# One encoder kernel, its DeltaNet core: the order of work on all engines set anew, the output copied out of its bank, the masks folded into the decay sums

## The chip, the core and the metric

The kernel is one program on one core of a Trainium2 chip. Five engines work side by side and meet only at semaphores: TensorE (PE, matrix products into PSUM), VectorE (DVE), ScalarE (ACT), GpSimd (POOL) and the queue of SyncE (SP), which issues the loads. An engine runs its own instructions strictly in the order in which they are written, so an instruction that waits holds back all that stand behind it. The metric is the time of one execution on the device in microseconds (us).

## What is computed

Two encoder layers on 256 tokens of width 2048, in float32. Layer 0 mixes tokens with a bidirectional gated DeltaNet (32 value heads on 16 key heads, two directions), layer 1 with a convolution module, and each is followed by a SwiGLU block. The change touches only the DeltaNet's recurrence. Cut to what matters (one direction; the other is the same on flipped time):

```python
g = jnp.cumsum(chunks(g), axis=-1)
decay = jnp.exp(jnp.where(incl, g[..., :, None] - g[..., None, :], -jnp.inf))
lower = jnp.where(strict, jnp.einsum('nbhid,nbhjd->nbhij', k_beta, k) * decay, 0.0)
sol = lax.linalg.triangular_solve(eye + lower, rhs, left_side=True, lower=True)
a_qk = jnp.einsum('nbhid,nbhjd->nbhij', q, k) * decay
# per chunk: v_new = u - w S ; o = (q exp(g)) S + a_qk v_new ; S = S cd + k_tail^T v_new
o = rmsnorm(o_f + o_b, norm_w) * jax.nn.silu(z)
return o.reshape(B, T, V_DIM) @ out_w
```

## The kernel before, in words

All projections before and after the core are dense products with split float32 weights (lines 651 to 670). Between them stands the **core**, a loop written out over 16 key heads. One "head" here is one key head with its two value heads and both directions, that is four problems `c` = 2 x direction + value head, over two blocks `t` of 128 tokens. With blocks of 128 the solve is done by block inversion: inverses of the 32x32 diagonal blocks (`inv`, made earlier, loaded per head) are joined to 64x64 and then to 128x128 inverses `t64`.

For each head the stages are, with the names that the prediction uses:

- **sums** (DVE, line 1415, 12 instructions): `exb` = row sums `rr` plus a column sum from `ncum`, cut off at 0. **exponentials** (ACT, line 1946, four for the keys `d0`, four for the queries `d1`): `dec` = exp(`exb`).
- **kq** (PE, line 885): k k^T and k q^T into the PSUM bank `psg[:, 0]`. **masks** (DVE, lines 1387 and 1389): `mk` = that bank times triangular 0/1 masks. **masked** (DVE, line 1395, four for keys, four for queries): `dec` times `mk`. **lm** (DVE, line 1406, four): the part of it that joins 32 to 64.
- **W** (PE, line 864), **wt** (ACT, line 1961, two copies), **tn** (line 908) and **t** (line 872) on PE, **tnb** (line 1445) and **t64** (line 1449) on DVE, **y** (line 940), **yb** (ACT, line 1983), **t2** (line 947), **t128** (ACT, line 1991, two copies): these join the inverses.
- **rv** (ACT, line 1979, eight): values times beta. **u0** (PE, line 856), **uu0** (ACT, line 1941, a copy), **X** (PE, line 895), **r2** (DVE, line 1422), **u1** (PE, line 856), **uu1** (ACT, line 1941): the solution of the first block, its effect on the second, the second.
- **o** (PE, line 925, 12 products, shown as x24): the output of both directions into the bank `ps_o`. **squares** (ACT, line 1956) read `ps_o`; **oms** (DVE, lines 1426 and 1429), 12 small operations on POOL (lines 2264 to 2270) for the inverse root, **og** (DVE, line 1439) reads `ps_o` again and multiplies by root and gate. **T** (PE, line 641) transposes `og`, **oT** (ACT, line 1986) stores it.

The order is written by hand. In its step `h` the loop makes the inverses of head h, solves and outputs head h-1, and finishes the statistics of head h-2; with two steps to drain it takes 18 steps. PE waits ahead of **o** for `og_done` of the head before, since `ps_o` is one bank:

```python
pe.wait_ge(uc_done, 2 * b + 2)
pe.wait_ge(aq_done, b + 1)
pe.wait_ge(og_done, b)
```

SP loads per head `rr` (1 MB, a broadcast), q and k, v, the gate z, and `inv` as eight small transfers (line 508), the last after `t64_done`, since `inv` is one buffer. The core is entered when the last gate product is copied out, and left when the last `oT` is stored; then the weights of the output projection are loaded into the buffers that the core had borrowed.

Of the kernel before, what the change touches and what calls it, by code (L numbers as in the profile page):

```python
# [64 lines left out]
def build(nc, x_in, c_in, ada_w, ada_b, norm_w, gdn_in_w, gdn_conv_w, gdn_A_log, gdn_dt_bias,  # L65
# [31 lines left out]
    with stack:  # L97
# [96 lines left out]
        masks = sb("masks", [P, 2, 2, 3, P], at=p2a)  # L194
# [8 lines left out]
        dec = sb("dec", [P, 2, 4, 2, 3, P], at=p2a)  # L203
        osq = sb("osq", [P, 4, P], at=p2a)
# [8 lines left out]
        sb("apart", [P, 756], at=p2a)  # L213
# [49 lines left out]
        ps_b = pst[:, 2:4, :].rearrange("p a (b m) -> p (a b) m", m=P)  # L263
# [75 lines left out]
        mk_done = sem("mk_done")  # L339
# [10 lines left out]
        u_done, uc_done = sem("u_done"), sem("uc_done")  # L350
# [23 lines left out]
        C_TRI, C_SINV, C_CONST = 5, 7, 22  # L374
# [41 lines left out]
        def _(sp):  # L416
# [94 lines left out]
            def core_loads(h):  # L511

                if h + 2 < HQ:
                    sp.wait_ge(kq_done, h + 2)
                    load_qk(h + 2)
                    sp.wait_ge(ex_done, h + 2)
                    load_rr(h + 2)
                if 1 <= h <= HQ:
                    if h > 1:
                        sp.wait_ge(og_done, h - 1)  # L520
                    else:
                        sp.wait_ge(z_out, 16 * NZ)
                    load_z(h - 1)
                if h + 1 < HQ:
                    sp.wait_ge(rv_done, 2 * (h + 1))
                    load_v(h + 1)
                    sp.wait_ge(t64_done, h + 1)
                    load_inv(h + 1)
# [29 lines left out]
            sp.wait_ge(inv_out, 48)  # L558
            sp.dma_start(x[:, :, :], x_in[0].rearrange("(t p) d -> p t d", p=P)).then_inc(x_land, 16)
            for h in range(HQ + 1):  # L560
                core_loads(h)
# [75 lines left out]
        def _(pe):  # L637
# [210 lines left out]
            def step(h):  # L848
                par, b = h % 2, h - 1
                M, A, B, C = h + 1 < HQ, h < HQ, 0 <= b < HQ, 0 <= h - 2  # L850
                q = 1 - par

                def u_stage(o):
                    for c in range(4):
                        t = o if c < 2 else 1 - o
                        i = mm(ps_a[:, c, :], t64[:, q, c, t, :], rv[:, q, o, c, :], start=True, stop=True)  # L856
                    i.then_inc(u_done, 1)

                def w_stage(d):

                    pe.wait_ge(lm_done, 2 * h + d + 1)
                    for c in (2 * d, 2 * d + 1):
                        for t in range(TT):
                            i = mm(ps_w[:, 2 * c + t, :], lm[:, c, t, :], inv[:, slot_of(0, c), t, :], start=True, stop=True)  # L864
                    i.then_inc(w_done, 1)

                def t_stage(d):

                    pe.wait_ge(wt_done, 2 * h + d + 1)
                    for c in (2 * d, 2 * d + 1):  # L870
# [4 lines left out]
                if B:  # L875
                    pe.wait_ge(rv_done, 2 * b + 1)
                    pe.wait_ge(t128_ok, 2 * (b + 1))
                    u_stage(0)
                if M:
                    pe.wait_ge(qk_land, 32 * (h + 2))  # L880
                    pe.wait_ge(mk_done, h + 1)
                    if h == 0:
                        pe.wait_ge(ps_read, S_GO)
                    for jt in range(2):
                        i = mm(psg[:, 0, jt, :], qk[:, 0, jt * P:(jt + 1) * P],  # L885
                               qk[:, :, :].rearrange("p k t -> p (k t)"), start=True, stop=True)
                    i.then_inc(kq_done, 1)
                if A:
                    pe.wait_ge(inv_land, 128 * (h + 1))
                    w_stage(0)  # L890
                    w_stage(1)
                if B:
                    pe.wait_ge(uc_done, 2 * b + 1)
                    for c in range(4):
                        i = mm(ps_b[:, c, :], dec[:, q, c, 0, 1, :], uu[:, 0, c, :], start=True, stop=True)
                    i.then_inc(x_done, 1)
                if A:
                    t_stage(0)
                    t_stage(1)
                if B:  # L900
                    pe.wait_ge(r2_done, 2 * (b + 1))
                    u_stage(1)
                if A:

                    for c in range(4):
                        f = first(c // 2)
                        for t in range(TT):
                            i = mm(ps_n[f, c % 2, t, :], inv[f, slot_of(1, c), t, f], wt[f, c, t, f], start=True, stop=True)
                    i.then_inc(tn_done, 1)
                if B:  # L910
# [17 lines left out]
                if C:  # L928
                    pe.wait_ge(og_done, h - 1)
                    pe.wait_ge(oT_done, h - 2)  # L930
                    for v in range(2):
                        for t in range(TT):
                            i = tr(ps_oT[:, v, t * P:(t + 1) * P], og[:, 2 * t + v, :])
                    i.then_inc(ot_done, 1)
                if A:
                    pe.wait_ge(tn_ok, 2 * (h + 1))
                    for c in range(4):
                        f, s = first(c // 2), second(c // 2)
                        for t in range(TT):
                            i = mm(ps_y[s, c % 2, t, :], dec[f, par, c, 0, 2 * t, s], tnb[f, c % 2, t, :], start=True, stop=True)  # L940
                    i.then_inc(y2_done, 1)
                    pe.wait_ge(y2_ok, h + 1)
                    pe.wait_ge(t64_done, h + 1)
                    for c in range(4):
                        f, s = first(c // 2), second(c // 2)
                        for t in range(TT):
                            i = mm(ps_n[f, c % 2, t, :], yb2[s, c % 2, t, :], t64[s, par, c, t, s], start=True, stop=True)
                    i.then_inc(t2_done, 1)
            for h in range(HQ + 2):
                step(h)  # L950
# [127 lines left out]
        def _(dve):  # L1078
# [296 lines left out]
            mkf = mk[:, :, :, :, :].rearrange("p d k s m -> p d k (s m)")  # L1375
            mmf = masks[:, :, :, :, :].rearrange("p d k s m -> p d k (s m)")
# [3 lines left out]
            def step(h):  # L1380
                par, b = h % 2, h - 1
                M, A, B, C = h + 1 < HQ, 0 <= h < HQ, 0 <= b < HQ, 0 <= h - 2
                p = 1 - par

                def mask(d):
                    kqf = kq0 if h < 0 else kqs
                    tt(mkf[:, d, :, d * P:(d + 2) * P], kqf[:, d], mmf[:, d, :, d * P:(d + 2) * P], MUL)
                    n = 2 - 2 * d
                    return tt(mkf[:, d, :, n * P:(n + 1) * P], kqf[:, 1 - d, :, (1 - d) * P:(2 - d) * P],
                              mmf[:, d, :, n * P:(n + 1) * P], MUL)  # L1390

                def masked(kind, done):
                    for c in range(4):
                        f = dec[:, par, c, kind].rearrange("p s m -> p (s m)")
                        i = tt(f, f, mk[:, c // 2, kind].rearrange("p s m -> p (s m)"), MUL)
                    i.then_inc(done, 1)

                if A:
                    dve.wait_ge(d0_done, h + 1)
                    dve.wait_ge(mk_done, h + 1)  # L1400
                    masked(0, la_done)
                    dve.wait_ge(la_done, h + 1)
                    dve.wait_ge(w_done, 2 * h)
                    for d in range(2):
                        for v in range(2):
                            i = tt(lm[:, 2 * d + v, :, :], dec[:, par, 2 * d + v, 0, 0:3:2, :],
                                   m64[:, d:d + 1, :].broadcast_to([P, TT, P]), MUL)
                        i.then_inc(lm_done, 1)
                if M:

                    dve.wait_ge(rr_land, 16 * (h + 2))
                    dve.wait_ge(d1_done, h + 1)
                    for c in range(4):
                        for seg, t, kind, tj in ((0, 0, 0, 0), (2, 1, 0, 1), (1, 1 - c // 2, 1, c // 2)):
# [883 lines left out]
```

## Time and profile before

| what | us |
|---|---|
| median of 3 runs (lowest, highest) | 3267.35 (3266.91, 3268.53) |
| the profiled execution, its own time | 3268.26 |
| its span | 3266.7 |
| PE busy in the span | 2953.7 |
| DVE busy | 2264.2 |
| ACT busy | 1275.6 |
| one head of the core, from one **o** to the next | 20.41 |
| first **W** of the core to the end of the last **oT** | 743.99 to 1083.06 |

Times inside the profile are counted from the start of the span. A row of instructions has its start, its length, engine, line and tiles; a `x24` behind it counts the instructions merged into it. A float32 product shows as two matmul records, so 12 products are x24. "PEclk" is the clock granted to TensorE, as a share of full speed: 1.00 is 2.4 GHz and 0.50 is 1.2 GHz.

### The profile page before, as it was taken

The page shows a single profiled execution, that of the slowest core. Times are in us where ns is not written, and L with a number is a line of the kernel's source. Part 1 is how long each engine was busy: PE and PEld are TensorE (multiplying, and loading weights), DVE is VectorE, ACT ScalarE, POOL GpSimd, SP SyncE. Part 2 cuts the span into 40 slices and gives each one's busy share as a digit, 9 for nine tenths or more (in the row PEclk, how much of TensorE's full clock was granted, in tenths as well). Part 3 has the DMA queues.
Part 4 walks back from the last instruction along what each step waited for, and adds up shares of the span by engine and source line. Part 5 has one row for each costly group of instructions (what it writes and reads, how often), then busy time and mean ns, then how long its engine had stood idle before and what let it go on. Part 6 is the DMA issues. An engine that isn't in the chain of part 4 may idle for free.

```text
span 3266.7 us, 37727 instructions
## 1 busy us (share of the span) xinstructions
PE 2953.7 (90%) x13796; PEld 2382.1 (73%) x13796; DVE 2264.2 (69%) x2388; ACT 1275.6 (39%) x1383; POOL 163.6 (5%) x313
## 2 busy tenths in 40 slices
PE   1699999997777698899999999799987999999998
PEld 1577778876777577788888888644576888888886
DVE  6588868967776478787877877529966655555555
ACT  2356634335554334333333333421144333333333
POOL 0011111320111000000000000000000000000000
PEclk8799999998998799999999999899998999999998
DMA  9666766674332598798888888354334766656653
GB/s 376 227 224 238 244 218 217 206 235 146 104 104 65 182 372 327 274 341 308 310 308 315 337 315 333 99 167 149 122 121 155 252 206 216 201 201 203 214 204 122
DMA packets 322173, 731.61 MB, mean 224 GB/s; under 512 B 48128, under 2 KB 64336, under 8 KB 293648
## 3 DMA queue, kind: packets, MB, share of 16 engines
q1 hardware_dynamic: 316256, 709.85, 61.5%
q0 software_dynamic: 5808, 20.35, 1.8%
q8 instruction: 62, 1.02, 0.1%
q14 instruction: 47, 0.39, 0.0%
HBM read 710.45 MB, written 19.69 MB: 224 GB/s over the span
## 4 chain that ended last, share of the span: by engine, by line
PE 82%; DVE 7%; DMA 4%; ACT 3%; issue 2%; POOL 2%; DVEq 0%; SPq 0%; ACTq 0%
PE psg L664 44%; PE psg L670 22%; PE psg L651 5%; DMA aring<-in_ada_w 3%; PE psn L925 2%; PE pst L641 1%; PE psn L691 1%; PE psg L864 1%; DVE wlo L1086 1%; PE psg L885 1%; PE psn L1049 1%; DVE y L1598 1%; PE psn L641 1%; DMA wraw<-in_gdn_out_w 1%; PE pst L856 1%
## 5 line engine op out<-in xcount | busy, mean ns | idle before, releaser
L1722 ACT ACTIVATE whi<-wraw 128x2048 fp32r<-128x2048 f32 x408 | 781.8, 1916 | 1319.7 <-PE psg L670 1163.6
L1086 DVE TENSOR_TENSOR wlo<-wraw,whi 128x2048 fp32r<-128x2048 f32 x408 | 935.2, 2293 | 482.9 <-ACT whi L1722 481.0
L664 PE MATMUL psg<-whi,h_hi 128*128 128x512 f32 x2304 | 731.3, 399 | 33.6 <-DVE h_lo L1678 13.2
L664 PE MATMUL psg<-whi,h_lo 128*128 128x512 f32 x2304 | 719.9, 394 | 0.0
L670 PE MATMUL psg<-wlo,h_hi 128*128 128x512 f32 x2304 | 572.1, 391 | 12.0 <-DVE wlo L1086 12.0
L664 PEld LDWEIGHTS psg<-whi,h_hi 128*128 128x128 f32 x2304 | 435.5, 191 | 127.9 <-issue 25.6
L670 PEld LDWEIGHTS psg<-wlo,h_hi 128*128 128x128 f32 x2304 | 433.6, 188 | 104.0 <-DVE wlo L1086 13.9
L664 PEld LDWEIGHTS psg<-whi,h_lo 128*128 128x128 f32 x2304 | 439.5, 191 | 93.9
L1096 DVE SCALAR_TENSOR_TENSOR aacc<-aring,cond,aacc 128x2048 f32<-128x2048 f32 x150 | 352.0, 2346 | 6.6 <-DMA aring<-in_ada_w 6.0
L651 PE MATMUL psg<-wraw,aring 128*128 128x512 f32 x512 | 221.1, 592 | 0.0
L664 PE MATMUL psg<-whi,g_hi 128*128 128x512 f32 x704 | 219.9, 394 | 0.0
L664 PE MATMUL psg<-whi,g_lo 128*128 128x512 f32 x704 | 219.3, 393 | 0.0
L651 PEld LDWEIGHTS psg<-wraw,aring 128*128 128x128 f32 x512 | 96.7, 190 | 118.6 <-issue 118.6
L670 PE MATMUL psg<-wlo,g_hi 128*128 128x512 f32 x704 | 173.9, 389 | 0.0
L664 PEld LDWEIGHTS psg<-whi,g_hi 128*128 128x128 f32 x704 | 134.1, 191 | 28.0
L664 PEld LDWEIGHTS psg<-whi,g_lo 128*128 128x128 f32 x704 | 133.9, 190 | 28.2
L1517 DVE TENSOR_TENSOR y<-psg,y 128x1024 f32<-128x1024 f32 x88 | 107.6, 1223 | 66.9 <-PE psg L670 66.1
L670 PEld LDWEIGHTS psg<-wlo,g_hi 128*128 128x128 f32 x704 | 132.2, 188 | 27.5
L1598 DVE SCALAR_TENSOR_TENSOR y<-glu,vec,y 128x242 f32 (+14 forms) x360 | 139.8, 475 | 0.0
L1310 DVE SCALAR_TENSOR_TENSOR cv<-pst,vec,cv 128x254 f32<-128x254 f32 (+1 forms) x256 | 117.3, 480 | 23.3 <-DVE cv L1310 1.7
L925 PE MATMUL psn<-wraw,dec 128*128 128x128 f32 x384 | 71.8, 372 | 45.2 <-DVE og L1439 45.2
L2251 POOL DMA_DIRECT2D d_cw<-cwc x4 | 4.7, 1178 | 2096.4 <-DVE cwc L1170 2095.5
(251 smaller groups left out, 2600.0 us busy)
## 6 DMA issues: line engine op xcount, KB each, us to landing
aring<-in_ada_w SPq DMA_DIRECT2D x192, 1024.0 KB, 7.0
wraw<-in_ffn_in_w SPq DMA_DIRECT2D x176, 1024.0 KB, 6.8
wraw<-in_gdn_in_w SPq DMA_DIRECT2D x96, 1024.0 KB, 5.1
wraw<-in_ffn_out_w SPq DMA_DIRECT2D x88, 1024.0 KB, 5.2
wraw<-in_cf_pw_w SPq DMA_DIRECT2D x48, 1024.0 KB, 5.5
wraw<-in_gdn_out_w SPq DMA_DIRECT2D x32, 1024.0 KB, 8.5
wraw<-d_rr SPq DMA_DIRECT2D x16, 1024.0 KB, 4.7
x<-in_x SPq DMA_DIRECT2D x2, 2048.0 KB, 9.2
```

The source lines that it names most:

```text
L641: return nc.tensor.transpose(dst, src, ident[:, :])
L651: i = mm(ps[:, t, :], a[:, kc, t * P:(t + 1) * P], wraw[:, slot, j * NSL:(j + 1) * NSL], start=first and j == 0, stop=last and j == len(kc ...
L664: mm(ps[:, t, 0:width], a[:, kc, t * P:(t + 1) * P], wh, start=first and j + n == 0, stop=False)
L670: i = mm(ps[:, t, 0:width], a_hi[:, kc, t * P:(t + 1) * P], wl, start=False, stop=last and j == len(kcs) - 1)
L691: i = mm(psn[:, 0, kc:kc + 1], acc[:, kc * P:(kc + 1) * P], ones[:, 0:1], start=True, stop=True)
L925: i = mm(ps_o[:, 2 * t + v, :], dec[:, q, c, 1, seg, :], uu[:, o, c, :], start=n == 0, stop=n == len(terms) - 1)
L1086: tt(wlo[:, j % 2, :], wraw[:, j % 4, :], whi[:, j % 2, :].bitcast(F32), SUB).then_inc(w_lo, 1)
L1096: stt(acc, ring[:, par, :], c, acc, MUL, ADD).then_inc(a_used, 1)
L1310: i = stt(dst, src, w, dst, MUL, ADD)
L1517: tt(yj, psg[:, (s0 + par) % 2], yj, ADD).then_inc(ps_read, 1)
L1598: i = stt(dst, src, w, dst, MUL, ADD)
L1722: av(whi[:, j % 2, :], wraw[:, j % 4, :], ACT.Copy).then_inc(w_hi, 1)
```

## The change

Only the core changes; the amount of PE work is the same. Five things are done.

**1. Five steps a head.** The statistics of the output move a step later, and the transpose **T** one more: step `s` of the new loop makes the inverses of head s, outputs head s-1, does the statistics of head s-2 and transposes head s-3. The first solution **u0** moves from the start of the next step to the end of its own. There are 19 steps on PE and ACT. In SP's queue the loads are in a new order, and the reload of `x` (2 MB), which stood ahead of the loop, stands behind step 3.

PE, one step in the middle of the core, before (the names are tiles: `psn<-wraw,dec` is **o**, `psn<-ident,og` is **T**, `psg<-wraw,lm` is **W**, `psg<-qk` is **kq**):

```order
L864 MATMUL psg<-wraw,lm 128x128 x8
L895 MATMUL pst<-wraw,dec 128x128 x4
L872 MATMUL psg<-wraw 128x128 x8
L856 MATMUL pst<-rv,t 128x128 x4
L908 MATMUL pst<-wraw 64x64 x8
L925 MATMUL psn<-wraw,dec 128x128 x12
L641 MATMUL psn<-ident,og 128x128 x4
L940 MATMUL pst<-tnb,dec 64x64 x8
L947 MATMUL pst<-t,yb 64x64 x8
L856 MATMUL pst<-rv,t 128x128 x4
L885 MATMUL psg<-qk 128x512 x2
```

PE, one step in the same place of the changed program:

```order
L869 MATMUL psg<-wraw,lm 128x128 x8
L641 MATMUL psn<-ident,og 128x128 x4
L882 MATMUL pst<-wraw,dec 128x128 x4
L893 MATMUL pst<-wraw 64x64 x8
L897 MATMUL psg<-wraw 128x128 x8
L903 MATMUL psg<-qk 128x512 x2
L911 MATMUL pst<-tnb,dec 64x64 x8
L856 MATMUL pst<-rv,t 128x128 x4
L922 MATMUL pst<-t,yb 64x64 x8
L940 MATMUL psn<-wraw,dec 128x128 x12
L856 MATMUL pst<-rv,t 128x128 x4
```

The same products stand in another order: **T** behind **W**, **tn** ahead of **t**, **kq** in the middle of the step, **u1** between **y** and **t2**, and **o** next to last.

DVE, one step before (`exb<-` are the sums, `og<-` the gated output):

```order
L1395 TENSOR_TENSOR dec<-dec,mk 128x384 x4
L1406 TENSOR_TENSOR lm<-dec,m 128x256 x4
L1415 TENSOR_SCALAR exb<-wraw,ncum 128x2x128 x12
L1422 TENSOR_TENSOR rv<-pst,rv 128x256 x2
L1426 TENSOR_SCALAR oms<-oms 128x4
L1429 TENSOR_SCALAR oms<-oms 128x4
L1395 TENSOR_TENSOR dec<-dec,mk 128x384 x4
L1439 SCALAR_TENSOR_TENSOR og<-psn,oms,zt 128x128 x4
L1445 TENSOR_TENSOR tnb<-pst,wraw 64x256 x2
L1449 TENSOR_TENSOR t<-psg,wraw 128x512 x2
L1387 TENSOR_TENSOR mk<-psg,masks 128x2x256
```

DVE, in the changed step, behind the sums (which are eight SCALAR_TENSOR_TENSOR and four TENSOR_SCALAR):

```order
L1385 TENSOR_SCALAR exb<-wraw,ncum 128x2x128
L1398 TENSOR_TENSOR dec<-dec,psg 128x2x256
L1398 TENSOR_TENSOR dec<-dec,psg 128x2x128
L1398 TENSOR_TENSOR dec<-dec,psg 128x2x256
L1398 TENSOR_TENSOR dec<-dec,psg 128x2x128
L1431 TENSOR_TENSOR tnb<-pst,wraw 64x256 x2
L1435 TENSOR_SCALAR oms<-oms 128x4
L1439 TENSOR_SCALAR oms<-oms 128x4
L1446 TENSOR_TENSOR rv<-rv,pst 128x256 x2
L1452 TENSOR_TENSOR t<-psg,wraw 128x512 x2
L1398 TENSOR_TENSOR dec<-dec,psg 128x2x256
```

Behind these rows come the rest of the keys, `lm`, and `og` as the last of the step. The masks are gone as instructions, and `og` no longer stands between the queries and `tnb`.

**2. The output is copied.** ACT copies `ps_o` to a buffer `os` as its first work of the next step; the squares and `og` read `os`. PE's wait for `og` ahead of **o** becomes a wait for that copy (`oc_ok`).

**3. Decay sums held twice.** `exb` has two halves, by the parity of the head, so the sums of a head wait for the query exponentials of the head before last.

**4. Masks as a bound.** A triangle `tri0` with 0 inside and -1000 outside is the upper bound of the sum, so that the exponential is 0 outside. `dec` is then multiplied by the products straight from PSUM.

**5. X goes to the bank `ps_a`**, from which `uu0` was copied, since `ps_b` shares its bank with **tn** and **y**. The factors -1 and the scale of the queries move from the masks into `m64`, **r2**, **yb** and the copy `os`.

```diff
-        mk = sb("mk", [P, 2, 2, 3, P], at=p2a)
-        exb = sb("exb", [P, 4, 2, 3, P], at=p2a)
+        exb = sb("exb", [P, 2, 4, 2, 3, P], at=p2a)
+        os = sb("os", [P, 4, P], at=p2a)
...
+            def decay_sums(h):
+                dve.wait_ge(rr_land, 16 * (h + 1))
+                if h > 1:
+                    dve.wait_ge(d1_done, h - 1)
+                for c in range(4):
+                    for seg, t, kind, tj in ((0, 0, 0, 0), (2, 1, 0, 1), (1, 1 - c // 2, 1, c // 2)):
+                        to, row = exb[:, h % 2, c, :, seg, :], rr[:, 2 * c:2 * c + 2, t * P:(t + 1) * P]
+                        col = ncum[:, kind, tj, c, h:h + 1]
+                        if seg == 1:
+                            i = ts(to, row, col, 0.0, ADD, MIN)
+                        else:
+                            i = stt(to, row, col, tri0[:, c // 2:c // 2 + 1, :].broadcast_to([P, 2, P]), ADD, MIN)
+                i.then_inc(ex_done, 1)
+
+            def decayed(h, kind, done):
+                kqf = kqs if h else kq0
+                for d in range(2):
+                    n = 2 - 2 * d
+                    f = dec[:, h % 2, 2 * d:2 * d + 2, kind].rearrange("p c s m -> p c (s m)")
+                    for to, kq in ((f[:, :, d * P:(d + 2) * P], kqf[:, d, kind, :]),
+                                   (f[:, :, n * P:(n + 1) * P], kqf[:, 1 - d, kind, (1 - d) * P:(2 - d) * P])):
+                        i = tt(to, to, kq.unsqueeze(1).broadcast_to(list(to.shape)), MUL)
+                i.then_inc(done, 1)
...
+                if C:
+                    act.wait_ge(o_done, g + 1)
+                    if g:
+                        act.wait_ge(og_done, g)
+                    av(os[:, :, :], ps_o, ACT.Copy, scale=float(P) ** -0.5).then_inc(oc_ok, 1)
...
                 if B:
-                    pe.wait_ge(uc_done, 2 * b + 2)
+                    pe.wait_ge(uc1_done, b + 1)
                     pe.wait_ge(aq_done, b + 1)
-                    pe.wait_ge(og_done, b)
+                    if b:
+                        pe.wait_ge(oc_ok, b)
...
+            def core_loads(s):
+                if s + 2 < HQ:
+                    sp.wait_ge(ex_done, s + 2)
+                    load_rr(s + 2)
+                if s + 1 < HQ:
+                    sp.wait_ge(rv_done, s + 1)
+                    load_v(s + 1)
+                    sp.wait_ge(t64_done, s + 1)
+                    load_inv(s + 1)
+                if s + 2 < HQ:
+                    sp.wait_ge(kq_done, s + 2)
+                    load_qk(s + 2)
...
+                sel(out=tri0[:, d, :], in_=tri0[:, d, :], compare_op=ALU.is_ge, fill=-1000.0, base=0,
+                    pattern=[[sign, P]], channel_multiplier=-sign)
```

## Rows read from the trace of the kernel before

**Rows 1.** Busy time of the engines in whole heads; columns: PE, PEld, DVE, ACT, POOL, clock, DMA.

```profile
799.58:820.00 20.42, 15.94 (x139) 14.34 (x138) 14.53 (x40) 10.90 (x32) 3.19 (x12) 0.92 0.36 104
```

**Rows 2.** Chain of work that ended last, one head: start, length, what.

```profile
785.95 4.54 PE psn L925 x24
790.49 0.44 PE psn L641 x4
790.93 0.91 PE pst L940 x16
...
792.29 0.98 PE pst L947 x16
...
794.22 1.13 PE pst L856 x8
795.35 1.72 PE psg L885 x4
797.06 1.78 PE psg L864 x16
798.85 0.91 PE pst L895 x8
...
806.36 4.54 PE psn L925 x24
```

**Rows 3.** The same chain in the second step, whose o waited for no og.

```profile
759.71 1.78 PE psg L864 x16
...
762.39 1.79 PE psg L872 x16
764.17 0.89 PE pst L856 x8
765.07 0.89 PE pst L908 x16
765.96 2.88 PE psn L925 x24
```

**Rows 4.** Busy time and clock, columns as in rows 1, of short stretches.

```profile
766.00:769.00 3.00, 3.00 (x28) 2.88 (x29) 2.94 (x6) 2.03 (x7) 0.00 (x0) 1.00 0.13 46
909.40:910.40 1.00, 1.00 (x6) 1.00 (x6) 1.00 (x3) 0.00 (x0) 0.00 (x0) 0.50 0.89 269
```

**Rows 5.** Who waited for whom in the core: us in total, times, longest.

```profile
PE psn L925 <- DVE og L1439: 45.2, 15, 3.1
PE pst L856 <- ACT t L1991: 15.4, 16, 1.0
```

**Rows 6.** Instructions in order of time, ACT, DVE and SP, in one head.

```profile
895.39 0.78 ACT L1991 ACTIVATE t<-pst 64x256 f32<-64x256 f32 x2 [0.56 <-PE pst L947]
896.19 1.76 ACT L1946 ACTIVATE dec<-exb 128x384 f32<-128x384 f32 x4
898.06 3.24 DVE L1415 TENSOR_SCALAR exb<-wraw,ncum 128x256 f32<-128x256 f32 x12 [2.66 <-ACT dec L1946]
910.33 0.68 DVE L1387 TENSOR_TENSOR mk<-psg,masks 128x512 f32<-128x512 f32 x1
910.45 3.79 SPq L508 DMA_DIRECT2D wraw<-d_inv  x8
912.38 1.97 DVE L1395 TENSOR_TENSOR dec<-dec,mk 128x384 f32<-128x384 f32 x4
```

**Rows 7.** The same view of DVE later, two SBUF tensors and a column scalar.

```profile
2199.87 6.36 DVE L1598 SCALAR_TENSOR_TENSOR y<-glu,vec,y 128x251 f32 x16
```

**Rows 8.** DMA issues of the core: count, KB each, median us to landing.

```profile
wraw<-d_inv SPq DMA_DIRECT2D x63, 32.0 KB, 2.0
```

**Rows 9.** The chain at the core's last W and its end.

```profile
1040.38 1.79 PE psg L864 x16
...
1075.16 1.15 ACT osq L1956 x8
...
1082.45 0.61 ACT oT L1986
```

More of the change, by code:

```diff
@@ L557, in _ @@
             load_rr(1)
[L558 to L561, printed above, removed]
+            for s in range(HQ + 1):
+                core_loads(s)
+                if s == 3:
+                    sp.wait_ge(inv_out, 48)
+                    sp.dma_start(x[:, :, :], x_in[0].rearrange("(t p) d -> p t d", p=P)).then_inc(x_land, 16)
             sp.wait_ge(oT_done, HQ)
@@ L927, in step @@
                     i.then_inc(o_done, 1)
[L928 to L934, printed above, removed]
-                if A:
[L936 to L950, printed above, removed]
+                if A:
+                    pe.wait_ge(rv_done, s + 1)
+                    pe.wait_ge(t128_ok, s + 1)
+                    u_stage(s, 0, u0_done)
+            for s in range(HQ + 3):
+                step(s)
             pe.wait_ge(oT_done, HQ)
@@ new lines, in keys @@
+            def keys(h):
+                dve.wait_ge(kq_done, h + 1)
+                dve.wait_ge(d0_done, h + 1)
+                decayed(h, 0, la_done)
+                dve.wait_ge(la_done, h + 1)
+                if h:
+                    dve.wait_ge(w_done, 2 * h)
+                for d in range(2):
+                    for v in range(2):
+                        i = tt(lm[:, 2 * d + v, :, :], dec[:, h % 2, 2 * d + v, 0, 0:3:2, :],
+                               m64[:, d:d + 1, :].broadcast_to([P, TT, P]), MUL)
+                    i.then_inc(lm_done, 1)
@@ new lines, in queries, with step @@
+            def queries(h):
+                dve.wait_ge(kq_done, h + 1)
+                dve.wait_ge(d1_done, h + 1)
+                decayed(h, 1, aq_done)
+            def step(s):
+                par, b, g = s % 2, s - 1, s - 2
+                M, A, B, C = s + 1 < HQ, s < HQ, 0 <= b < HQ, 0 <= g < HQ
+                if M:
+                    decay_sums(s + 1)
+                if A:
+                    if s:
+                        queries(s)
+                    dve.wait_ge(tn_done, s + 1)
+                    for d in range(2):
+                        f, slot = first(d), slot_of(0, 2 * d)
+                        i = tt(tnb[f], ps_n[f], inv[f, slot:slot + 2, :, f], ADD)
+                    i.then_inc(tn_ok, 1)
+                if C:
+                    dve.wait_ge(osq_done, g + 1)
+                    ts(oms[:, 1, :], oms[:, 0, :], 1.0 / P, RMS_EPS, MUL, ADD).then_inc(oms_done, 1)
+                    dve.wait_ge(oms_done, 2 * g + 1)
+                    if g:
+                        dve.wait_ge(ors_done, 12 * g)
+                    ts(oms[:, 2, :].bitcast(I32), oms[:, 1, :].bitcast(I32), -0.5, float(0x5f3759df), MUL, ADD
+                       ).then_inc(oms_done, 1)
@@ L1459, in _ @@
+            decay_sums(0)
+            keys(0)
+            queries(0)
             dve.wait_ge(inv_out0, 48)
@@ L1461, in _ @@
             dve.wait_ge(kk_out, 16 * 4 * 4)
-            for h in range(HQ + 2):
-                step(h)
+            dve.wait_ge(z_out, 16 * NZ)
+            for s in range(HQ + 2):
+                step(s)
             dve.wait_ge(oT_done, HQ)
@@ L1968, in step @@
-                if B:
-                    solution(1)
+                if C:
+                    act.wait_ge(oc_ok, g + 1)
+                    if g:
+                        act.wait_ge(oms_done, 2 * g)
+                    for n in range(4):
+                        i = av(osq[:, n, :], os[:, n, :], ACT.Square, accum_out=oms[:, 0, n:n + 1])
+                    i.then_inc(osq_done, 1)
+                if E:
+                    act.wait_ge(ot_done, e + 1)
+                    av(oT[:, 2 * e:2 * e + 2, :], ps_oT, ACT.Copy).then_inc(oT_done, 1)
@@ L2000, in _ @@
             act.wait_ge(kk_out, 16 * 4 * 4)
-            for h in range(HQ + 2):
-                step(h)
+            for s in range(HQ + 3):
+                step(s)
             hi(G_GO, G_GO)
```

308 lines of the change are left out of this document (130 added, 178 removed).

## The prediction

> **What bounds the kernel now.** I read the core first, since only it changes: its heads take 20.41 us each, from one **o** to the next [rows 2], and PE is busy for 15.94 us of such a stretch, DVE for 14.53, ACT for 10.90 [rows 1]. So no engine is full. The chain of waits says who holds the period: PE itself at every stage but three. The PE stages of one head add up, in the order of the chain, to 4.54 (**o**) + 0.44 (**T**) + 0.91 (**y**) + 0.98 (**t2**) + 1.13 (**u0**) + 1.72 (**kq**) + 1.78 (**W**) + 0.91 (**X**) [rows 2] + 1.79 (**t**) + 0.89 (**u1**) + 0.89 (**tn**) [rows 3] = 15.98, which is the busy time of rows 1. The 4.4 us left are three waits of every head: **o** for **og** 45.2/15 = 3.0, **u0** for the copies **t128** 15.4/16 = 1.0 [rows 5], and **t2** for **yb**, from the end of **y** at 790.93 + 0.91 to 792.29, 0.5 [rows 2].
>
> The first of these waits costs more than itself. **o** takes 4.54 us in a head that waited [rows 2] but 2.88 us in the second step, which waited for nothing [rows 3]. The granted clock tells why: it is at 0.50 (1.2 GHz) within an **o** that followed such a wait, and at 1.00 (2.4 GHz) in the undisturbed one [rows 4]. Waits of 0.5 and 1.0 us are followed by stages at their full-clock length (**t2** 0.98, **u0** 1.13) [rows 2]. So the wait for **og** costs 3.0 + (4.54 - 2.88) = 4.7 us a head, of 20.4.
>
> **The change, part by part.**
>
> *The copy and the later statistics.* **o** of head s-1 now waits for the copy of head s-2, which ACT makes early in the step, some 10 us ahead. The chain squares, oms, POOL, og stays as long as it was but ends in a later step, where only **T** of the step after next needs it. Gain 4.7 us a head; added are 0.60 us of ACT for the copy (a copy of 128x512 from PSUM, like `oT` [rows 9]), beside PE's work. If the cover were gone, the copy would cost its 0.60.
>
> *The other two waits.* **u1** (0.89) now runs between **y** and **t2**, longer than the 0.5 us that **yb** needs; **o** (2.88) runs between **t2** and **u0**, longer than the 1.0 us of **t128**. Gain 0.5 + 1.0 = 1.5. What is late next: **X** stands 1.78 + 0.44 us behind the end of **u0** and needs **uu0**. ACT, from the end of **o**, does `d1` 1.76 [rows 6], `os` 0.60, **uu0** 0.60, so **uu0** is ready at about 3.0; **X** may start at 1.13 + 1.78 + 0.44 = 3.35. It fits by 0.3.
>
> *PE after it.* 15.98 - 1.66 = 14.3 us a head at full clock. This is the floor.
>
> *DVE.* Removed: the masks, 912.38 - 910.33 = 2.05 us, and the masked products, 2 x 1.97 = 3.94, and the old sums, 3.24 [rows 6]. Added: the products straight from PSUM. They have the shapes of the masks (512, 256, 512, 256 elements, one operand from the same bank) and are needed once for the keys and once for the queries, so 2 x 2.05 = 4.10. The new sums: four as before at 3.24/12 = 0.27, and eight with two tensors from SBUF and a column scalar. The nearest row has 16 such of 251 elements in 6.36 us, 0.40 each [rows 7]. 4 x 0.27 + 8 x 0.40 = 4.28. DVE is then busy for 14.53 - 2.05 - 3.94 - 3.24 + 4.10 + 4.28 = 13.7 us. From below the new sums cannot be under the 3.24 of the simpler ones; from above they cost twice the old 0.27 each, 8 x 0.54 + 1.08 = 5.4, DVE 14.8. I take 4.28: that row differs from the new one only in the broadcast operand.
>
> On this the Trainium skill speaks against the change. Its page "VectorE: DVE Perf Modes", section "Mode 2×_2P — use both read ports for one tensor", says that a float32 operation with one SBUF tensor may use both read ports and run at two elements a cycle, which one with two tensors cannot. Taken as a factor of two it gives the 5.4 us above; the rows have 0.40 against 0.27, since much of so short an instruction is fixed.
>
> *Double `exb`.* Before, the sums waited 2.66 us for the exponentials [rows 6]. With two halves they wait for nothing near. It moves no engine that is the bound by itself, but without it DVE would not fit into 14.3.
>
> *ACT.* 10.90 + 0.60 = 11.5 us busy. But ACT stands in a ring with PE: end of **o**, all of ACT's step up to **uu1** but not **t128** (0.78 [rows 6]), then **o** again: 11.5 - 0.78 + 2.88 = 13.6, with two hand-overs 13.8. Under PE, by half a microsecond.
>
> *SP and the load of `inv`.* One buffer, loaded between **t64** and the next **W**. From the end of **t64**, 3.79 us of issue [rows 6] and 2.0 to the landing [rows 8]: 5.8. In a step that starts with **W**, **t** ends at 1.78 + 0.44 + 0.91 + 0.89 + 1.79 = 5.8; DVE adds 1.2 to 1.3 for **t64**, and if it comes late from **r2** up to 1.5 more: end 7.1 to 8.6, landing 12.9 to 14.4. **W** is due at 14.3. This is the closest of all, and it is new: before, the issue began at 910.45 [rows 6], 9.1 us ahead of the next **W** (which stood 11.1 us behind the start of **o** [rows 2], near 919.6). At zero to 0.1 us of waiting I leave it inside the joints below. `rr` is asked for after the sums and has some 10 us to land; q and k are issued behind `inv` now, and are needed most of a step later.
>
> *Joints.* Three loops (PE 14.3, DVE 13.7, ACT and PE 13.8) and the load at 14.4 touch each other, each hand-over costing 0.05 to 0.1. I take 0.3 for them, between 0 and 1: a **period of 14.6 us**.
>
> *Start.* The first **W** waits for the same: sums of head 0, exponentials, keys. DVE now makes the queries of head 0 before it goes on (+2 us), but loses the masks. The second step's **W** started at 759.71 [rows 3]; it hangs on **t64** of head 0 and the `inv` load, and I keep 759.7, 1 us either way. The 2 MB for `x` no longer go ahead of the first loads; they land beside step 4.
>
> *End.* Before, from the last head's **W** to the last `oT`: 1082.45 + 0.61 - 1040.38 = 42.7 us [rows 9]. After: the rest of that step 14.6; then **uu0** 0.6, **X**, **r2** 0.8, **u1**, **uu1** 0.6, **o** with the hand-overs, 7 us at full clock, 12 at half, taken 9.0; then `os` 0.6 and from squares to `oT` as now, 1083.06 - 1075.16 = 7.9. Sum 32.1. The third pipeline stage costs one step of latency at the end, and that is in it. The load of the next weights behind it stays.
>
> *Sum.* 759.7 + 14 x 14.6 + 32.1 = 996.2 against 1083.1: 86.9 us gained. The profiled execution took 3268.26, so 3181.4; the median of the runs shown is 0.9 lower, so **3180.5**.
>
> **The rivals.** Each microsecond on the period is 15 us of time.
>
> *B, DVE becomes the bound.* If the new sums cost 5.4, or the products from PSUM more than the masks did, DVE needs 14.8, and with its own waits (for `d0`, for POOL between oms and og) 15.2 to 16. Speaks for it: DVE is at 13.7 of 14.6 in strict order. Against: rows 7. Time 3190 to 3202.
>
> The price of 5.4 is the one that the rule of the skill's VectorE page gives if it is taken as a plain factor of two.
>
> *C, the load of `inv` becomes the bound.* If it lands 2 us later than its median, PE idles some 1 to 2 us ahead of every **W**, and the clock may fall again as it did behind the wait for **og**, 1.7 more: period 17 to 18, time 3217 to 3232. Speaks for it: eight small issues in series, next to no slack. Against: the 1 MB of `rr` is no longer in flight at the same time.
>
> *D, slower than before.* The place is PE's order itself: eleven stages, nearly each behind another engine's semaphore. If the small waits between them kept the granted clock at 0.50 for the whole step, the 14.3 us of work would take 28.6: 3180.5 + 15 x 14.3 = 3395. It decides against the change from the point where a step has more than 2 x (20.4 - 14.6) = 11.6 us at half clock. Against it: the short waits of today are followed by stages at full length.
>
> *E, it does not do what it says.* DVE's fixed order could pass the old wait on: **kq** now waits for the queries, **y** for `tnb`, both behind the sums. If DVE were a whole chain behind, the period would stay near 20 and the time near 3262.
>
> **How the numbers follow.** Forecast (period 14.1 to 15): 0.58, 3173 to 3187. B: 0.22. C: 0.12. D: 0.03. E: 0.05, of which a fifth ends within 0.2% of before. The range takes in the forecast with the period at 14.1 and a short end (3168), all of B, and what lies between B and C up to a period of 16.7 (3212); left out are the rest of C, D and E. A measurement of this kernel tells about 0.2%, 6.5 us, from no change. Faster by more: 0.95; within: 0.01; slower: 0.04.
>
> **What would show it.** In the changed profile: **o** at about 2.9 us with a granted clock near 1.00 through the core; no wait of PE for **og** except at the end; heads at 14.6 us; the new sums at 0.40 each and products from PSUM like the masks; PE ahead of **W** waiting for the load by tenths. If instead DVE is busy without a gap and **kq** or **y** wait for it, B is right; if **W** waits for a DMA by a microsecond or more, C. The forecast is wrong if **o** stays at 4.5 without a wait ahead of it: then its length was not the clock's, and 1.7 x 15 = 25 us of the gain are missing.

## The result

The changed kernel takes 3178.53 us (median of 4 runs, 3175.08 to 3181.21) against 3267.75 us for the kernel before (4 runs): ratio 0.9725, 95% interval 0.9713 to 0.9737, 89 us less. The profiled execution took 3177.12 us, 91.1 less than the one of before. Two executions ran quite otherwise, one of `b_order` (3859 us, mean granted clock 0.74) and one of the kernel before (6827 us), and stand in none of the ratios.

Nearly all of the gain is in the core: from the first **W** to the end of the last **oT** it took 743.99 to 1083.06 before and takes 742.40 to 991.10 now, 90.4 us less. The chain of work that ended last, one step in the middle of the changed kernel (start, length, engine, tile, line, count):

```profile
844.50 1.79 PE psg L869 x16
846.28 0.44 PE psn L641 x4
846.72 1.01 PE pst L882 x8
847.73 0.89 PE pst L893 x16
848.62 1.98 PE psg L897 x16
850.60 1.72 PE psg L903 x4
852.32 0.89 PE pst L911 x16
853.21 1.09 PE pst L856 x8
854.30 0.89 PE pst L922 x16
855.20 2.88 PE psn L940 x24
858.07 0.89 PE pst L856 x8
858.96 1.79 PE psg L869 x16
```

Where the products of [rows 2] have room between them, for the waits of [rows 5] and for **yb**, there is PE alone: each row begins where the one before ends, 14.46 us from **W** to **W** against 20.41. **o** (now line 940) has 2.88 us as in [rows 3], not the 4.54 of [rows 2]. The busy times and the clock of the next step (PE, PEld, DVE, ACT, POOL, clock, DMA, as in [rows 1]) say the same:

```profile
858.96:873.43 14.47, 14.47 (x139) 12.70 (x138) 13.56 (x37) 11.17 (x35) 2.38 (x12) 1.00 0.51 143
```

PE is busy for all of the step at a clock of 1.00, where [rows 1] had 15.94 of 20.42 at 0.92. Who waited for whom on PE in the core answers to [rows 5]. This is all of PE's waiting above 1 us:

```profile
PE psg L869 <- DVE lm L1410: 13.0, 1, 13.0
PE psn L641 <- DVE og L1464: 6.5, 1, 6.5
PE psg L869 <- DMA wraw<-d_inv: 1.9, 2, 1.6
PE pst L856 <- DVE rv L1446: 1.1, 1, 1.1
```

A wait for **og** is left once, at the end; the first line is the start, and the third is the load of the inverses, 1.6 us of it ahead of the second **W** and 0.3 us ahead of the one at 815.42. In order of time, DVE and SP in one step answer to [rows 6]:

```profile
861.79 1.94 DVE L1398 TENSOR_TENSOR dec<-dec,psg 128x512 f32<-128x512 f32 x4
866.92 4.17 SPq L506 DMA_DIRECT2D wraw<-d_inv  x8
867.66 1.95 DVE L1398 TENSOR_TENSOR dec<-dec,psg 128x512 f32<-128x512 f32 x4 [0.77 <-ACT dec L1949]
872.04 0.87 DVE L1387 SCALAR_TENSOR_TENSOR exb<-wraw,ncum,tri 128x256 f32<-128x256 f32 x2
```

The products straight from PSUM take 1.95 us a kind. The sums begin at 872.04, one step earlier at 857.58, and the queries behind them at 861.79: 4.21 us. SP issues the load of the inverses from 866.92 to 871.09, with the next **W** at 873.43. DVE's one wait in the step is for the key exponentials, 0.77 us. The core's last **W** and its end answer to [rows 9]:

```profile
960.22 2.02 PE psg L869 x16
...
977.85 4.59 PE psn L940 x24
...
990.49 0.61 ACT oT L1981
991.12 13.65 DMA wraw<-in_gdn_out_w
```

### The profile page after: what moved, and what is told of

Read it like the earlier page. It is cut to its first block, busy times and chain, and to the rows that moved or that the text cites. A ratio compares the mean times of both kernels' runs of the same rounds, so it can differ in the third digit from the quotient of the medians.

```text
span 3175.5 us, 37732 instructions
## 1 busy us (share of the span) xinstructions
PE 2926.3 (92%) x13796; PEld 2354.4 (74%) x13796; DVE 2248.5 (71%) x2324; ACT 1280.5 (40%) x1399; POOL 149.5 (5%) x306
## 4 chain that ended last, share of the span: by engine, by line
PE 83%; DVE 7%; DMA 5%; ACT 3%; issue 2%; SPq 0%; DVEq 0%; POOL 0%; ACTq 0%
PE psg L664 44%; PE psg L670 22%; PE psg L651 5%; DMA aring<-in_ada_w 3%; PE pst L641 1%; DMA wraw<-in_gdn_out_w 1%; PE psn L940 1%; PE psn L691 1%; PE psg L897 1%; DVE wlo L1084 1%; PE psg L869 1%; PE psn L1047 1%; PE pst L856 1%; DVE y L1609 1%; PE psn L641 1%
## 5 line engine op out<-in xcount | busy, mean ns | idle before, releaser
L670 PEld LDWEIGHTS psg<-wlo,h_hi 128*128 128x128 f32 x2304 | 433.5, 188 | 103.7 <-DVE wlo L1084 13.7
L664 PE MATMUL psg<-whi,o_hi 128*128 128x512 f32 x256 | 83.3, 408 | 25.4 <-DVE o_lo L1482 19.9
```

What stands on the lines that cost most here:

```text
L664: mm(ps[:, t, 0:width], a[:, kc, t * P:(t + 1) * P], wh, start=first and j + n == 0, stop=False)
L670: i = mm(ps[:, t, 0:width], a_hi[:, kc, t * P:(t + 1) * P], wl, start=False, stop=last and j == len(kcs) - 1)
```

## The experiments

The theory before them: the gain is the removed wait for **og** with the slow clock behind it (4.7 us a head), and the two short waits (1.5). The rivals: **o** was long for another reason; one part of the change alone would do it; DVE, not PE, sets the step. "Step" is always from **W** to **W** on PE. Every experiment was run in alternation with the kernel before, whose medians lay between 3264.7 and 3270.0 us.

### Was the long o the clock's?

```diff
                     pe.wait_ge(aq_done, b + 1)
+                    if h >= 2:
+                        pe.wait_ge(oT_done, h - 2)
+                        for _ in range(13):
+                            mm(ps_oT[:, 0, 0:P], ident[:, :], ident[:, :], start=True, stop=True)
                     pe.wait_ge(og_done, b)
```

> The kernel before with 13 idle products (128x128 of the identity, into the free half of the output bank) ahead of PE's wait for og, about 2.9 us of PE work in the 3.0 us of waiting. Theory (the clock): PE is never idle long, so the granted clock stays at 1.00 and o takes 2.9 us in place of 4.54; 1.66 us a head over 14 heads, 23 us less than before, about 3245 us, although PE does more. Rival (o is long because it meets DVE and ACT at PSUM or SBUF): o stays at 4.5 us and the time at 3268 us.

Measured: 3261.2 us, ratio 0.9967 (0.9956 to 0.9978), 9 us less. Two steps from the chain, the first up to its **kq** (line 885) only; line 916 is the filler, line 929 **o**:

```profile
866.33 2.79 PE psn L929 x24
...
874.00 3.39 PE psg L885 x4
...
883.64 3.10 PE psn L916 x26
886.74 2.79 PE psn L929 x24
...
894.39 1.72 PE psg L885 x4
```

**o** is 2.79 us long in both steps: with PE busy ahead of it its length is that of full clock. That part of the theory holds and its rival falls. But the gain is less than half of 23 us. In the first of the two steps **kq** takes 3.39 us, twice its 1.72, and the granted clock from 874.00 to 877.30 is 0.51. From **W** to **W** seven of the twelve steps from 775.21 us on are 20.2 to 20.4 us, as without the filler, and five are 18.7: together 8.9 us less than twelve of 20.42. The slow clock had moved: once **o** was protected, it fell on **kq** in more than half the steps. **kq** stands behind **t2** and **u0**, that is behind the waits of 0.5 and 1.0 us.

The kernel before shows the same where no wait for **og** came first, in its first two steps (chain of its trace, `before`):

```profile
757.06 2.65 PE psg L885 x4
773.86 2.78 PE psg L885 x4
```

**u0** ahead of them has 1.87 and 1.74 us instead of 1.13, and the granted clock from 757.10 to 759.60 is 0.66. So the prediction's reading, that the two short waits are followed by stages of full length, holds for the later heads of that trace and not for these two.

### The copy of the output alone

```diff
+                    av(os[:, :, :], ps_o, ACT.Copy).then_inc(oc_ok, 1)
+                    act.wait_ge(oc_ok, h - 1)
...
-                        i = av(osq[:, n, :], ps_o[:, n, :], ACT.Square, accum_out=oms[:, 0, n:n + 1])
+                        i = av(osq[:, n, :], os[:, n, :], ACT.Square, accum_out=oms[:, 0, n:n + 1])
...
-                    pe.wait_ge(og_done, b)
+                    if b:
+                        pe.wait_ge(oc_ok, b)
```

> The kernel before with one part of the change alone: ACT copies the output out of its bank, squares and og read the copy, o waits for the copy. Order, masks and decay sums as before. Theory: the wait for og ahead of o (3.0) and the slow clock behind it (1.66) go, the waits for yb and t128 (1.5) stay: period 20.42 - 4.7 = 15.7 us, 15 heads, 3198 us (3190 to 3208). Rival (the wait only moves): T stands right behind o in the same step and needs og of that step, so PE waits there up to 3 us and the clock still falls: 3240 us or more.

Measured: 3225.49 us, ratio 0.9871 (0.9855 to 0.9888), 45 us less where 70 were expected. The waits of DVE in the core between 765 and 960 us:

```profile
DVE og L1442 <- POOL oms L2277: 25.6, 11, 2.3
```

In the kernel before, DVE stood just as long ahead of **og**:

```profile
907.19 1.12 DVE L1439 SCALAR_TENSOR_TENSOR og<-psn,oms,zt 128x128 f32<-128x128 f32 x4 [2.34 <-POOL oms L2270]
```

Steps are 16.95 us long in the middle (839.77 to 856.70 to 873.65), and the chain of such a step runs over DVE from **og** to the sums and over POOL back to **og**: 14.4 us of DVE's work and 2.3 of waiting for POOL's root, in DVE's fixed order, the rest hand-overs. Both sides named beforehand were off: the wait ahead of **o** was gone, **T** did not take its place, and DVE became the bound. The two short waits of PE stood in every step (0.5 and 1.0 us, 12 times between 765 and 960 us), and yet the granted clock was 1.00 over the whole of that stretch, with **kq** at full length in each step.

### The statistics later, on DVE and in T

On top of `b_copy`: **og** last in DVE's step, **T** one step later, `z` loaded behind v and `inv`.

```diff
-                if C:
-                    pe.wait_ge(og_done, h - 1)
-                    pe.wait_ge(oT_done, h - 2)
+                if 0 <= h - 3:
+                    pe.wait_ge(og_done, h - 2)
+                    pe.wait_ge(oT_done, h - 3)
```

> The kernel before with the copied output as in b_copy, and besides og moved to the end of DVE's step, T one step later, and the load of z behind v and inv. PE's order of the other stages, the masks and the one buffer of decay sums stay. In b_copy DVE held the period: it stood 2.4 us a head in front of og, waiting for POOL's root. Theory (that wait in DVE's order took the gain of the copy): DVE now works through POOL's root, PE is the bound with 14.3 of work and 1.5 of its own two waits, period 15.8 to 16.0, about 3203 us. Rival (the masks or the single buffer of sums hold DVE anyway): period near b_copy's 16.95 and 3220 to 3226 us.

Measured: 3212.49 us, ratio 0.9835 (0.9815 to 0.9856), between the 3203 of the theory and the 3220 of the rival. DVE no longer waits for POOL, and PE's only waits in the middle are its own two. From two neighbouring steps of the chain (line 858 is **u0**, 887 **kq**):

```profile
870.38 1.72 PE psg L887 x4
...
884.95 1.23 PE pst L858 x8
886.19 3.31 PE psg L887 x4
```

A step whose **kq** takes 1.72 is 15.7 us (856.24 to 871.94); one whose **kq** takes 3.31 is 17.4 (871.94 to 889.33), and nine of the eleven steps from 786.92 to 974.32 are of that kind (the expectation below for the next kernel counts one more of each). From 886.20 to 889.40 the granted clock is 0.52. So in this kernel the two short waits, which I had put down at 1.5 us, cost 1.5 plus a dip of 1.7 in most steps. In `b_copy`, with the same two waits and a longer step, they cost no dip; why the one and not the other, no run here shows.

### PE's order on top of it

```diff
                 if B:
                     pe.wait_ge(r2_done, 2 * (b + 1))
-                    u_stage(1)
...
                     i.then_inc(y2_done, 1)
+                if B:
+                    u_stage(1)
+                if A:
                     pe.wait_ge(y2_ok, h + 1)
```

and **o** moved from ahead of **y** to behind **t2**, **T** ahead of **y**, and ACT's **uu1** behind **yb**.

> b_late with PE's order changed on top: u1 moved from ahead of tn to between y and t2, T ahead of y, and o moved from ahead of y to behind t2 (ahead of u0); ACT makes uu1 behind yb. The masks as instructions and the one buffer of decay sums stay as before. In b_late the steps are 15.7 us where the clock stays up and 17.4 us in 10 of the 12 whole steps, where kq runs at half clock behind the two short waits (0.5 and 1.0 us). Theory (those two waits cost their 1.5 and the dip of 1.7, and the new order takes away both): steps of 14.5 to 15.2 us without dips, DVE with 14.5 of work now as close a bound as PE; about 3187 us. Rival (the order alone is not enough without the second buffer of sums and the cheaper masks): DVE or the ring through the exponentials holds 16 us or more, 3200 us or above.

> The same kernel as b_order, for a profile in which the clock is not held down for the whole execution. From its time, 28 us below b_late: steps of 15.0 to 15.8 us, no half-clock stage behind y and t2. If the theory of b_order holds, PE's two short waits are gone and what is left above 14.46 are waits of PE for DVE; if the rival does, most steps still have a dip.

Measured: 3184.88 us, ratio 0.9750 (0.9734 to 0.9766), and 3183.22 us, ratio 0.9745 (0.9716 to 0.9773), in the second. The profile of the second, chain of one step:

```profile
882.28 1.86 DVE dec L1400 x4
...
884.50 0.44 DVE tnb L1443
884.99 0.96 PE pst L923 x16
885.95 1.09 PE pst L858 x8
887.04 0.89 PE pst L933 x16
887.93 2.88 PE psn L951 x24
890.80 0.89 PE pst L858 x8
891.70 1.72 PE psg L887 x4
```

No dip is left: the clock is 1.00 in each of nine stretches of 18 us from 775 to 937, **kq** has 1.72, and steps are 14.96 us. What holds them now is DVE (queries, then `tnb`, for which **y** waits 0.7 us a step). The theory holds. Against the changed kernel's 14.46 there remain 0.50 us a step, 7.5 us in all, for the parts that this kernel lacks, taken together: the masks as a bound, the second buffer of sums, and the finer order. In time that is 3184 against 3178.

### The second buffer of sums

```diff
-                if h > 1:
-                    dve.wait_ge(d1_done, h - 1)
+                if h > 0:
+                    dve.wait_ge(d1_done, h)
...
-                        to, row = exb[:, h % 2, c, :, seg, :], rr[:, 2 * c:2 * c + 2, t * P:(t + 1) * P]
+                        to, row = exb[:, 0, c, :, seg, :], rr[:, 2 * c:2 * c + 2, t * P:(t + 1) * P]
```

> The changed kernel with one buffer for the decay sums in place of two: the sums of a head wait for the query exponentials of the head just before. Theory: the sums start 2.3 us later in every step, which is more than DVE's 0.8 us of slack, and the ring o, exponentials, sums, queries, r2, u1, uu1 becomes the bound: period 15.5 in place of 14.46, about 3193 us. Rival (the second buffer is not needed, PE is the bound with room): 3179 us.

Measured: 3196.34 us, ratio 0.9775 (0.9759 to 0.9792), 18 us above the changed kernel. PE's waits in the core, and DVE's for its sums between 765 and 960 us:

```profile
PE psg L903 <- DVE dec L1398: 10.8, 11, 1.2
PE psg L869 <- DMA wraw<-d_inv: 7.2, 7, 1.9
...
DVE exb L1387 <- ACT dec L1949: 29.0, 12, 4.2
```

DVE is late by more than its room: **kq** waits for the queries, and, since **t64** is late too, **W** waits for the inverses. Steps vary from 14.5 to 17.4, on average 15.97 (twelve from 776.22 us on), against the 15.5 expected.

That is more than the 14.96 of `b_order`, which has one buffer too and its masks besides. There the sums hardly wait (`b_order2`):

```profile
DVE exb L1420 <- ACT dec L1952: 3.6, 13, 1.1
```

2.4 us a step here against 0.3 there: so much of the need for the second buffer comes with the changed order itself, in which the query exponentials are ACT's last work of a step, behind **o**, and the next sums DVE's first. What the parts are worth depends on the order in which they are added.

### og back ahead of o

```diff
                     if b:
                         pe.wait_ge(oc_ok, b)
+                        pe.wait_ge(og_done, b)
```

> The changed kernel with the wait for og put back ahead of o, beside the wait for the copy (og of the head two before, last of DVE's step). By the trace o starts at 869.59 and that og ends at 872.1, so PE waits 2.5 us a step. Theory (waits of this length bring the clock down): 2.5 + up to 1.7 us a step, period 18.5 to 19, about 3240 us. Rival (the clock plays no part): period 17.0 and 3216 us, o at 2.9 us.

Measured: 3219.9 us, ratio 0.9843 (0.9827 to 0.9860), 41 us above the changed kernel. The waits, and the busy times and clock of two stretches of 18 us:

```profile
PE psn L941 <- DVE og L1465: 30.4, 12, 2.6
...
811.00:829.00 18.00, 15.65 (x131) 13.93 (x130) 12.09 (x32) 11.17 (x33) 2.37 (x12) 0.88 0.61 211
...
901.00:919.00 18.00, 15.38 (x146) 13.57 (x146) 14.33 (x38) 12.05 (x36) 2.37 (x12) 1.00 0.39 118
```

The wait is 2.5 us on average as foreseen, but most steps are 17.12 us (849.78 to 866.90) with **o** at 2.93: they lose the wait and nothing more. Four steps are 18.3 to 20.0, and in those **o** is slow: behind the same wait of 2.6 us the granted clock is 0.50 from 807.80 to 813.00 and 1.00 from 863.30 to 866.00. The time fits the rival's numbers (17.0, 3216, 2.9) and not the theory's 3240, though the four slow steps show that the clock does play a part: a wait of 2.6 us did not bring it down in most steps, although in `b_late` two waits of 0.5 and 1.0 close to each other did in most. What of a step's idle time decides is not settled by these runs.

### How much room is there?

Three kernels change one load or one cost of the changed kernel. `a_nobound` uses `ts` with the bound 0 for all sums and so leaves the masks out of the computation:

```diff
-                        if seg == 1:
+                        if True:
```

> The changed kernel with all twelve decay sums in the cheap form with one tensor and the bound 0, that is, the triangle is left out and the masks are missing from the computation. DVE has 8 x 0.13 = 1.0 us less to do a step. Theory (PE is the bound, DVE has room): the period stays at 14.46 and only the start gains about 1 us: 3177 us. Rival (DVE's order holds the period): 1.0 us a step less, 3163 us.

> The changed kernel itself, beside the two that follow: 3178 us.

Measured in one comparison: 3177.45 us for the changed kernel (3173.83 to 3181.89), 3171.24 for `a_nobound` (3169.67 to 3172.60). The steps of the latter are 14.46 and 14.47 us throughout, from 766.15 to 954.20 us; DVE's saved microsecond became waiting:

```profile
DVE dec L1398 <- ACT dec L1949: 17.1, 14, 1.3
DVE tnb L1431 <- PE pst L893: 7.0, 13, 1.2
```

So the 6 us between the medians are not in the steps. The two profiled executions, 3171.22 and 3181.89 us, differ at the start: the first sums begin at 728.29 and at 732.93 us (the row sums' load lands earlier or later), and the step that starts with the second **W** takes 14.02 us in one and 16.67 in the other, whose **W** ran at half clock. About 1 us can be put down to the cheaper first sums; for the rest of the 6 us no run shows the cause. The start scatters in the changed kernel too: its second **W** stands at 757.56 in the trace of 3177.12 us and at 760.79 in that of 3181.89, and the steps behind them take 14.02 and 16.67 us. That is probably why its runs spread over 8 us.

`a_dve` goes the other way, with one more DVE operation a step:

```diff
+                    for n in range(1):
+                        i = tt(scr[:, :, :], ident[:, :].unsqueeze(1).broadcast_to([P, 5, P]),
+                           ident[:, :].unsqueeze(1).broadcast_to([P, 5, P]), ADD)
```

> The changed kernel with one more DVE operation a step, behind og: 640 elements, about 0.73 us, into a buffer that nobody reads; that is about what the masks folded into the sums save DVE. Theory (PE is the bound and DVE has 0.8 to 0.9 us of room): period 14.46 to 14.6, at most 2 us more, 3180 us. Rival (DVE's order holds the step too): 0.7 a step, 3188 us.

Measured: 3176.76 us (3171.52 to 3181.10), no difference from the changed kernel. Most steps stay at 14.46 us, four are 14.7 to 15.4, and PE's waits for the inverses come to 1.6 us in all. So DVE has room for about this operation and hardly more. It is about what the folded masks save DVE, so with the sums held twice they may be worth little; that is argued, since no run puts the masks back as instructions.

`a_qkfirst` asks for `inv` behind q and k:

```diff
+                    if s + 2 < HQ:
+                        sp.wait_ge(kq_done, s + 2)
+                        load_qk(s + 2)
                     sp.wait_ge(t64_done, s + 1)
                     load_inv(s + 1)
```

> The changed kernel with the load of q and k ahead of that of inv in SP's queue: the last of the eight inv transfers is asked for some 0.9 us later. Theory (the inverses land 0.8 us before W, so the load is close but not the bound): W waits 0.1 to 0.3 us a step, 2 to 5 us more, 3181 us. Rival (much room): 3178 us; rival (no room, the load already sets the step): 0.9 a step, 3191 us.

Measured: 3184.13 us (3182.81 to 3187.58), 6 us more, a little above the 2 to 5 expected. PE now waits for the inverses in seven steps:

```profile
PE psg L869 <- DMA wraw<-d_inv: 6.0, 7, 1.3
```

So the load has room, but in about half of the steps less than 0.9 us, and it is the next bound.

### A version that beats both

Behind the core stand 13.65 us (13.69 before) for weight tiles that are asked for only when the last `oT` is stored. Three of them can be loaded as soon as their buffer is free:

```diff
+                if s == HQ - 1:
+                    sp.wait_ge(ex_done, HQ)
+                    load_w(G_GO + 1, (G_GO + 1) % 4, rows4(gdn_out, KT * P, 0))
+                    sp.wait_ge(t64_done, HQ)
+                    load_w(G_GO + 2, (G_GO + 2) % 4, rows4(gdn_out, 2 * KT * P, 0))
                 core_loads(s)
...
+            sp.wait_ge(o_done, HQ)
+            load_w(G_GO + 3, (G_GO + 3) % 4, rows4(gdn_out, 3 * KT * P, 0))
             sp.wait_ge(oT_done, HQ)
```

> The changed kernel with three of the four first weight tiles of the output projection asked for as soon as the borrowed buffer is free (sums of the last head, t64 of the last head, last o) and not behind the last oT. Theory: the chain has 13.65 us of waiting for these loads behind the core, of which some 1.5 us of splitting remain: 11 to 13 us less, 3166 us. Rival (the splits of weights and of the output on ACT and DVE, or the later tiles' loads, hold the product anyway): 0 to 4 us less.

Measured: 3166.44 us (3162.69 to 3169.82), ratio to the kernel before 0.9685 (0.9667 to 0.9703), 11 us below the changed kernel in the same comparison. The chain behind the last transpose:

```profile
995.04 1.91 ACT whi L1741
997.05 4.49 DVE wlo L1092 x2
1001.54 1.15 DVE o_lo L1490
1002.82 6.51 PE psg L672 x16
```

The wait for the load is gone; the splits of the weights and of the output are left.

## Why the prediction was right, point by point

- **What bounds the kernel** (PE's chain with three waits in it): right for the period of 20.4 us.
- **o at full clock**, 2.88 in place of 4.54: right, shown by the changed trace and by `b_fill`.
- **The copy and the later statistics, 4.7 us a head**: right for the two together, wrong as I then expected of the copy alone in `b_copy`. I had added up DVE's work (14.53) without the 2.34 us that it stood in front of **og**. In the old order that wait is inside DVE's own ring, and the copy does not remove it. Alone the copy gave 3.5 us of the step's 5.95.
- **The other two waits, 1.5 us**: undersized where a dip comes with them. They cost 1.5 and a dip of 1.7 in most steps of `b_late`, in seven of twelve of `b_fill` and in the first two steps of the kernel before, whose trace I had; in `b_copy` they cost 1.5 at most. The sum came out all the same, because it charged one dip a head, to the wait for **og**, and the changed order has none at all. With PE's order kept that one dip would in most steps only have moved from **o** to **kq**, as `b_late` shows.
- **PE 14.3, joints 0.3**: 14.46 measured, so 0.14 in place of 0.3. The joints are not waits but PE's stages behind stages of another shape: **t** 1.98 in place of 1.79, **u1** 1.09 for 0.89, **X** 1.01 for 0.91, less 0.24 at **u0** and 0.09 at **t2**.
- **DVE 13.7**: 13.56. The sums 4.21 against 4.28 taken, the products 1.95 a kind against 2.05. The plain factor of two, 5.4 us for the sums, is refuted by the rows of the changed kernel as it was by [rows 7]. So for instructions as short as these, the rule of the Trainium skill ("VectorE: DVE Perf Modes", section "Mode 2×_2P — use both read ports for one tensor") gives the direction of this cost and not its size.
- **ACT ring 13.8, room 0.5**: ACT was busy for 11.17 us against 11.5 and did not hold the step; it keeps DVE waiting 0.77 us for the key exponentials.
- **The load of the inverses**: right as the closest; PE waited for it 0.3 us once in the middle, and `a_qkfirst` bounds its room at under 0.9 us in seven steps.
- **Start and end**: the second step's **W** at 757.56, 2.1 us earlier than taken, but at 760.79 in the other trace of the same kernel, so this term is within its scatter. From the last **W** to the last `oT` 30.9 us against 32.1: the last step has no **kq** (1.72) and was counted as a whole one; **o** of the last head ran at half clock with 4.59.
- **Sum**: 757.56 + 202.66 (14 steps) + 30.9 = 991.1 against 996.2 foreseen, 3177.1 against 3181.4 for the profiled execution and 3178.5 against 3180.5 for the median. The miss is 2.1 at the start, 1.7 in the period and 1.2 at the end, all one way. That the median came closer than the profiled execution is luck: it was taken 0.9 us below it and lies 1.4 above.
- **Rivals**: B (DVE the bound) did not come, and `a_dve` puts its distance at about 0.73 us of work a step; DVE does hold `b_copy` and, by 0.5, `b_order`. C did not come but is the nearest. D and E did not come.

What each part is worth, in steps: 20.42 before; 16.95 with the copy; 15.7, or 17.4 with a dip, with the later statistics; 14.96 with PE's order; 14.46 with the sums held twice, the cheaper masks and the finer order. In time: 3268, 3225, 3212, 3184, 3178.

## What to carry to other kernels

When a wait is taken off one engine, add up every other engine's step with its own waits in it, in its fixed order, and not only its busy time: in `b_copy` a step in which DVE is busy for 14.4 us and stands for 2.3 takes 16.95. A long reduction chain over other engines is hidden by putting other work of the waiting engine between its start and its end, and by letting the result be used a step later. And behind an idle stretch of PE look at the length of the next stages, in every step and not in one: a wait of 3.0 us cost 4.7.

## What the runs showed that I had not expected

The half clock is not tied to the long wait. With PE filled ahead of **o**, in `b_fill`, seven of twelve steps were long, with a half-clock stage behind waits of 0.5 and 1.0 us (3.39 us for **kq** where 1.72 is full speed), and in `b_late` nine of eleven; in `b_copy`, with the same two waits in each step, none was. In `a_og` a single wait of 2.6 us was followed by **o** at 2.93 us, full speed, in most steps. In `b_fill` and `b_late` such a dip cost 1.7 us. What decides is left open. In the changed kernel, with no such waits, the granted clock is 1.00 over the whole of 765 to 960 us.
